# Block 3 of a three-block kernel: the cache of split weight tiles goes, and five multiplications of each recurrence element move from VectorE to GpSimd

## The reference, cut to what matters

```
h = x @ w_in + b_in                       # 1024 -> 4608 columns: 4 x 512 attention, 5 x 512 recurrence
q_a, k_a, v_a, g_a, q_h, z_fwd, z_bwd, i_h, g_h = split(h)
o_a = neighbourhood_attention(q_a, k_a, v_a, rpb) * silu(g_a)     # 8 heads, windows on a grid of 64 columns
for z in (z_fwd, z_bwd):                                          # 4 heads, forwards and backwards
    f = lb + (1 - lb) * sigmoid(z);  k = 1 - f;  b = cumsum(log f)
    o += hgrn2_chunk_scan(q_h, k, i_h, log f)
    # S_t = diag(f_t) S_(t-1) + k_t outer v_t;  o_t = S_t^T q_t, done in chunks:
    # a[t, s] = sum_d q[t, d] * exp(b[t, d] - b[s, d]) * k[s, d]  for s <= t
y = concat(o_a, rms(o) * gain * silu(g_h)) @ w_out + b_out
out = layer_norm(x * alpha + y)
```

## Time and profile before

| | us |
|---|---|
| median of 3 runs (lowest, highest) | 4557.69 (4555.84, 4560.75) |
| the profiled execution: its time, its span | 4560.75, 4558.9 |
| busy over the span: PE, DVE, ACT, POOL | 4255.9, 2695.0, 1808.8, 654.2 |
| mean granted clock of PE | 0.969 |

### The profile page before, as it was taken

One profiled execution on the slowest core, in us unless ns is written; L12 is line 12 of the kernel. 1 busy time (PEld: TensorE's weight loads), 2 busy tenths in 40 slices (PEclk: granted clock), 3 DMA queues, 4 the chain that ended last, 5 costly groups with the idle time before them and its releaser, 6 DMA issues.

```text
span 4558.9 us, 62157 instructions
## 1 busy us (share of the span) xinstructions
PE 4255.9 (93%) x24340; PEld 3457.5 (76%) x24372; DVE 2695.0 (59%) x4207; ACT 1808.8 (40%) x3435; POOL 654.2 (14%) x305
## 2 busy tenths in 40 slices
PE   7999999999899989999899979888999999899689
PEld 4888888889788877788677758767887777777467
DVE  5688888871566533044467667466354564376665
ACT  5111111111566631122466547455353453266453
POOL 2111111110333311111022112322000000000111
PEclk9999999999999999999999989999999999999789
DMA  4111111122544421111589862577664655654653
GB/s 170 51 51 51 51 51 51 51 72 91 188 131 128 129 92 49 65 59 63 188 259 290 272 255 93 177 226 257 221 206 166 198 185 169 205 188 150 207 188 129
DMA packets 515372, 663.95 MB, mean 146 GB/s; under 512 B 60348, under 2 KB 407296, under 8 KB 491658
## 3 DMA queue, kind: packets, MB, share of 16 engines
q1 hardware_dynamic: 466046, 576.89, 38.8%
q10 hardware_dynamic: 49036, 83.09, 4.9%
HBM read 442.24 MB, written 217.65 MB: 145 GB/s over the span
## 4 chain that ended last, share of the span: by engine, by line
PE 81%; DMA 6%; DVE 5%; SPq 3%; ACT 3%; issue 2%; POOL 1%; ACTq 0%; DVEq 0%; POOLq 0%
PE ps L226 10%; PE ps L227 10%; PE ps L228 10%; PE ps L3624 3%; PE ps L3625 3%; PE ps L3626 3%; PE ps L251 3%; PE ps L252 3%; PE ps L253 3%; PE ps L3744 2%; DMA w_split_tiles<-w 1%; PE ps L3713 1%; PE ps L239 1%; PE ps L240 1%; PE ps L241 1%
## 5 line engine op out<-in xcount | busy, mean ns | idle before, releaser
L226 PE MATMUL ps<-hh,wsplit 128*128 128x512 f32 x2048 | 821.7, 401 | 8.2 <-DVE hl L1376 4.2
L227 PE MATMUL ps<-hl,wsplit 128*128 128x512 f32 x2048 | 809.7, 395 | 0.0
L228 PE MATMUL ps<-hh,wsplit 128*128 128x512 f32 x2048 | 808.6, 395 | 0.0
L952 DVE SCALAR_TENSOR_TENSOR conv_acc<-conv_in,pcol,conv_acc 128x1024 f32<-128x1024 f32 x480 | 687.4, 1432 | 14.8
L226 PEld LDWEIGHTS ps<-hh,wsplit 128*128 128x128 f32 x2048 | 387.1, 189 | 102.3 <-issue 7.4
L227 PEld LDWEIGHTS ps<-hl,wsplit 128*128 128x128 f32 x2048 | 390.8, 191 | 91.7 <-issue 4.3
L228 PEld LDWEIGHTS ps<-hh,wsplit 128*128 128x128 f32 x2048 | 389.3, 190 | 89.3
L218 POOL TENSOR_TENSOR wsplit<-wraw,wsplit 128x1024 fp32r<-128x1024 f32 x72 | 204.9, 2856 | 1341.1 <-ACT wsplit L213 1341.1
L3624 PE MATMUL ps<-h_hi,w 128*128 128x512 f32 x896 | 374.9, 418 | 4.4 <-DVE h_lo L3422 4.4
L3625 PE MATMUL ps<-h_lo,w 128*128 128x512 f32 x896 | 357.7, 399 | 0.0
L3626 PE MATMUL ps<-h_hi,w 128*128 128x512 f32 x896 | 356.3, 398 | 0.0
(11 more groups left out here) (389 smaller groups left out, 8871.4 us busy)
## 6 DMA issues: line engine op xcount, KB each, us to landing
w<-w_split_tiles SPq DMA_DIRECT2D x108, 1024.0 KB, 5.4
wraw<-in_w_in SPq DMA_DIRECT2D x72, 512.0 KB, 3.8
w_split_tiles<-w SPq DMA_DIRECT2D x36, 1024.0 KB, 6.5
sh<-hy_ak ACTq DMA_DIRECT2D x48, 512.0 KB, 3.9
g_tiles<-b_ost SPq DMA_DIRECT2D x80, 256.0 KB, 5.5
w_raw<-in_w_in SPq DMA_DIRECT2D x36, 512.0 KB, 4.3
wo_raw<-in_w_out SPq DMA_DIRECT2D x32, 512.0 KB, 5.5
sh<-hy_ad ACTq DMA_DIRECT2D x32, 512.0 KB, 9.5
```

The lines of the kernel that those rows point to most:

```text
L226: e.matmul(p[:, :], wh, c.HH[tb][:, k, :], start=k == 0, stop=False)
L227: e.matmul(p[:, :], wh, c.HL[tb][:, k, :], start=False, stop=False)
L228: t = e.matmul(p[:, :], wl, c.HH[tb][:, k, :], start=False, stop=k == 7)
L952: e.scalar_tensor_tensor(v, a[:, h * 1024 + j:(h + 1) * 1024 + j], c.convw(j, ch), v, ALU.mult, ALU.add) \
```

## The change

The DRAM tensor of split tiles, its stores and its semaphores go. All 144 tiles are loaded raw and split by ScalarE and GpSimd, where it was 36. The five multiplications by k of each element go from VectorE to GpSimd, with a semaphore of their own (`rec_pool`) for which TensorE's products, and VectorE's next write of k, wait. The diff, without hunks that only delete declarations:

```diff
--- before.py
+++ after.py
...
@@ -2672,13 +2670,9 @@
         L.last_unit[n] = u
         if n >= 4:
             after(last[n - 4], "ld", n)
-            if n < 36:
-                before(last[n - 4] + 2, "split", n)
+            before(last[n - 4] + 2, "split", n)
 
     L.begin = [36 * tb for tb in range(4)]
-    L.first_with = {L.tiles[n][2]: n for n in range(36)}
-    for n in range(36):
-        after(max(last[n] - 1, 0), "w_st", n)
 
     L.units = [(tb, hd, d, h) for tb in range(4) for hd in range(4) for d in range(2) for h in range(2)]
     for n, (tb, hd, d, h) in enumerate(L.units):
@@ -2779,7 +2773,7 @@
     end = max(max(pre), max(post)) + 1
     L.order = []
     rank = {"split": 0, "log": 1, "div": 2, "el": 3, "sg": 4, "att_o": 1.5,
     for s in range(end):
-            "ld": 0, "w_st": 0.2, "val": 1, ...
+            "ld": 0, "val": 1, ...
         L.order += sorted(pre.get(s, []), key=lambda x: rank.get(x[0], 20))
         if s in L.begin:
@@ -2808,29 +2802,12 @@
 
 
 def w3_load(e, c, n):
-    L, s = c.b3, w3_slot(n)
+    L = c.b3
     if n >= 4:
         e.wait_ge(*L.done[L.last_unit[n - 4]])
-    if 4 <= n < 40:
-        e.wait_ge(*L.w_st[n % 4][n - 4])
-    if n < 36:
-        col = tile_col(L, n)
-        e.dma_start(L.Wraw[:, s, 1024:2048].rearrange("p (k n) -> p k n", k=8),
-                    c.A["w_in_3"][0][:, col:col + 128].rearrange("(k p) n -> p k n", p=128)).then_inc(*L.w_ld[n % 4].up(n))
-    else:
-        at = L.first_with[L.tiles[n][2]]
-        e.wait_ge(*L.w_st[at % 4][at])
-        e.dma_start(L.W[:, s, :].bitcast(F32), L.WD[at]).then_inc(*L.w_ld[n % 4].up(n))
-
-
-def w3_store(e, c, n):
-    L = c.b3
-    e.wait_ge(*L.lo[n])
-    e.dma_start(L.WD[n], L.W[:, w3_slot(n), :].bitcast(F32)).then_inc(*L.w_st[n % 4].up(n))
-
-
-def w3_ready(L, n):
-    return L.lo[n] if n < 36 else L.w_ld[n % 4][n]
+    col = tile_col(L, n)
+    e.dma_start(L.Wraw[:, w3_slot(n), 1024:2048].rearrange("p (k n) -> p k n", k=8),
+                c.A["w_in_3"][0][:, col:col + 128].rearrange("(k p) n -> p k n", p=128)).then_inc(*L.w_ld[n % 4].up(n))
 
 
 def w3_high(e, c, n):
@@ -2999,8 +2976,6 @@
         k = s[0]
         if k == "ld":
             w3_load(e, c, s[1])
-        elif k == "w_st":
-            w3_store(e, c, s[1])
         elif k == "row_ld" and s[1] >= 2:
             row_ld(s[1])
         elif k == "turn_x" and s[1] >= 4 and s[1] % 4 < 2:
@@ -3309,7 +3284,7 @@
             e.wait_ge(*c.by_act[u])
             e.tensor_scalar(f, f, L.lbv[:, a + 16 + hd:a + 17 + hd], L.lbv[:, a + 12 + hd:a + 13 + hd], ALU.mult, ALU.add).then_inc(*L.f_d.up(((tb, hd), "f", d)))
             if tb or hd:
-                e.wait_ge(*L.r_dve[first_of(tb, hd) - 4 + 2 * d + 1, "ke"])
+                e.wait_ge(*L.r_pool[first_of(tb, hd) - 4 + 2 * d + 1, "ke"])
             e.wait_ge(*L.f_d[(tb, hd), "f", d])
             e.tensor_scalar(L.KK[:, d, :], f, -1.0, 1.0, ALU.mult, ALU.add).then_inc(*L.f_d.up(((tb, hd), "k", d)))
         elif kind == "rq":
@@ -3371,15 +3346,10 @@
         to = L.QE[:, qs, :] if d else L.KE[:, s, :]
         e.tensor_tensor(v3(to, 128), v3(w, 128), end, op).then_inc(*L.r_dve.up((n, "dif", "l")))
         for lv, (B, x, kd, qsl, ksl) in enumerate(lvs):
-            e.wait_ge(*L.r_act[n, "k", lv])
-            e.tensor_tensor(kd[:, :, ksl], kd[:, :, ksl], v3(k, B)[:, :, ksl], ALU.mult).then_inc(*L.r_dve.up((n, "k", lv)))
             e.wait_ge(*L.r_act[n, "q", lv])
             e.tensor_tensor(x[:, :, qsl], x[:, :, qsl], v3(q, B)[:, :, qsl], ALU.mult).then_inc(*L.r_dve.up((n, "q", lv)))
         e.wait_ge(*L.r_act[n, "qd"])
-        e.tensor_tensor(L.KD[:, s, :], L.KD[:, s, :], k, ALU.mult).then_inc(*L.r_dve.up((n, "kd")))
         e.tensor_tensor(L.QD[:, s, :], L.QD[:, s, :], q, ALU.mult).then_inc(*L.r_dve.up((n, "qd")))
-        e.wait_ge(*L.r_act[n, "ke"])
-        e.tensor_tensor(L.KE[:, s, :], L.KE[:, s, :], k, ALU.mult).then_inc(*L.r_dve.up((n, "ke")))
         e.wait_ge(*L.r_act[n, "qe"])
         e.tensor_tensor(L.QE[:, qs, :], L.QE[:, qs, :], q, ALU.mult).then_inc(*L.r_dve.up((n, "qe")))
 
@@ -3587,6 +3557,16 @@
         k = s[0]
         if k == "split":
             w3_low(e, c, s[1])
+        elif k == "el":
+            n = s[1]
+            k = inputs_of(L, n)[1]
+            for lv, (B, x, kd, qs, ks) in enumerate(levels(L, n)):
+                e.wait_ge(*L.r_act[n, "k", lv])
+                e.tensor_tensor(kd[:, :, ks], kd[:, :, ks], v3(k, B)[:, :, ks], ALU.mult).then_inc(*L.r_pool.up((n, lv)))
+            for name, t in (("kd", L.KD), ("ke", L.KE)):
+                v = t[:, n % 2, :]
+                e.wait_ge(*L.r_act[n, "qd" if name == "kd" else "ke"])
+                e.tensor_tensor(v, v, k, ALU.mult).then_inc(*L.r_pool.up((n, name)))
         elif k == "wo_split":
             for q in range(s[1], s[1] + 4):
                 e.wait_ge(*L.wo_hi[q])
@@ -3618,15 +3598,14 @@
         e.wait_ge(*c.by_dve["x", 4 * tb + 3, 1])
         s = w3_slot(n)
         if u[0] == "col":
-            e.wait_ge(*w3_ready(L, n))
+            e.wait_ge(*L.lo[n])
             for k in range(8):
                 wh, wl = L.W[:, s, k * 128:(k + 1) * 128], L.W[:, s, 1024 + k * 128:1024 + (k + 1) * 128]
                 e.matmul(p[:, :], wh, L.HH[:, k, :], start=k == 0, stop=False)
                 e.matmul(p[:, :], wh, L.HL[:, k, :], start=False, stop=False)
                 t = e.matmul(p[:, :], wl, L.HH[:, k, :], start=False, stop=k == 7)
         else:
-            e.wait_ge(*w3_ready(L, n))
-            e.wait_ge(*w3_ready(L, n + 1))
+            e.wait_ge(*L.lo[n + 1])
             for i in range(2):
                 ts, out = slice(128 * (u[5] + i), 128 * (u[5] + i) + 128), p[:, 256 * i:256 * i + 256]
                 for k in range(8):
@@ -3644,6 +3623,7 @@
         for lv, (B, x, kd, qs, ks) in enumerate(levels(L, n)):
             h = B // 2
             e.wait_ge(*L.r_dve[n, "q", lv])
+            e.wait_ge(*L.r_pool[n, lv])
             for bl in range(256 // B):
                 i = bl * B % 128
                 k0 = i + ks.start if B > 32 else i
@@ -3654,12 +3634,13 @@
         e.matmul(p, c.zb[:, 0:128], c.zb[:, 0:256], start=False, stop=True)
         p = both[:, 256:512]
         e.wait_ge(*L.r_dve[n, "qd"])
+        e.wait_ge(*L.r_pool[n, "kd"])
         for j in range(2):
             ps = slice(j * 128, (j + 1) * 128)
             t = e.matmul(p[:, ps], L.KD[:, s, ps], L.QD[:, s, ps], start=True, stop=True)
         t.then_inc(*L.r_pe.up((n, "diag")))
         p = take_bank(e, c, ("kv", n), L.rb)
-        e.wait_ge(*L.r_dve[n, "ke"])
+        e.wait_ge(*L.r_pool[n, "ke"])
         for j in range(2):
             ps = slice(j * 128, (j + 1) * 128)
             t = e.transpose(p[:, ps], L.KE[:, s, ps], c.ident)
```

More of the change, by code:

```diff
@@ L2560, in b3_layout @@
     L.QED, L.KVD, L.OD = dram("chain_q_rows", 4, 128, S_LEN), dram("chain_kv_rows", 4, 128, S_LEN), dram("rec_o_rows", 4, 128, S_LEN)
-    L.WD = c.nc.dram_tensor("w3_split_tiles", (36, 128, 2048), F32, kind="Internal").ap()
     L.RD, L.BD = dram("rpb_rows", 120, 128), dram("bias_rows", 2, 4, 128, 1152)
@@ L2572, in b3_layout @@
     L.hi, L.lo, L.done = sig("w3_hi"), sig("w3_lo"), sig("b3_projected")
-    L.w_st = [dsig(f"w3_split_st{i}") for i in range(4)]
     L.tr, L.h_hi = sig("x2_turned"), sig("h3_hi")
@@ L2580, in b3_layout @@
     L.f_a, L.f_d = sig("forget_by_act"), sig("forget_by_dve")
-    L.r_pe, L.r_act, L.r_dve = sig("rec_pe"), sig("rec_act"), sig("rec_dve")
+    L.r_pe, L.r_act, L.r_dve, L.r_pool = sig("rec_pe"), sig("rec_act"), sig("rec_dve"), sig("rec_pool")
     L.qe_st, L.kv_st, L.o_st = [dsig(f"chain_q_st{i}") for i in range(4)], [dsig(f"chain_kv_st{i}") for i in range(2)], [dsig(f"rec_o_st{i}") for i in range(2)]
@@ L2781, in b3_order @@
     rank = {"split": 0, "log": 1, "div": 2, "el": 3, "sg": 4, "att_o": 1.5,
-            "ld": 0, "w_st": 0.2, "val": 1, "turn": 2, "qk": 3, "bias": 4, "out": 0.3, "state": 0.4, "prod": 3.5, "y_ld": 7, "ch_o": 8, "sq": 8.2, "o_root": 8.4, "chain": 9, "o_sum": 9.5, "o": 10, "o_end": 11, "y_split": 12, "o_norm": 13, "fin": 19, "o_st": 24, "x_ld": 25, "ch_ld": 26, "values": 27}
+            "ld": 0, "val": 1, "turn": 2, "qk": 3, "bias": 4, "out": 0.3, "state": 0.4, "prod": 3.5, "y_ld": 7, "ch_o": 8, "sq": 8.2, "o_root": 8.4, "chain": 9, "o_sum": 9.5, "o": 10, "o_end": 11, "y_split": 12, "o_norm": 13, "fin": 19, "o_st": 24, "x_ld": 25, "ch_ld": 26, "values": 27}
     for s in range(end):
```

## The result

| | before | changed |
|---|---|---|
| median of 4 runs, us | 4558.28 | 4593.75 (4592.61 to 4598.52) |
| the profiled execution, its span | 4560.75, 4558.9 | 4597.2, 4595.4 |
| time block 0 | 312.4 | 289.8 |
| time block 1 | 289.1 | 297.5 |
| time block 2 | 334.2 | 343.8 |

The ratio is 1.0078, 95% interval 1.0065 to 1.0090: slower by 35 us, as forecast (4599, +41). The block times are read from the trace, from the first matmul of the in-projection in one time block to the first of the next (the last: to the end of slot 143). By this measure the blocks of the kernel before begin at 2915.4, 3227.8, 3516.9 and 3851.1 us, and its 144 slots take 1302 us, 9.0 each. Before time block 0 the changed kernel has 0.9 us more.

The account below looks back on a forecast made before the run. TensorE sets the pace, with SyncE's queue, held by stores, pacing block 0. Terms −20 + 21 + 39 − 3 + 4 = +41 us gave 4602 against 4560.75, or 4599 against the median; range 4534 to 4650.

Parts of the forecast that it names:

- A, stores: Block 0: the 36 stores go, raw loads no longer wait for them; −20 us, bounds −34 and −5.
- R4: Rival, block 0: stores were no limit, bursts keep tiles late, gain only −5 us; 4614, chance 0.08.
- Price on GpSimd: Small multiplications on GpSimd: 0.43 us for 128 columns, 0.71 for 256, 2.7 us an element.
- The element: Element on VectorE beside GpSimd's multiplications: +1.1 us each, bounds −1.7 and +2.4.
- The subtract: GpSimd's 1024-column subtract holds VectorE up to 2.4 us; in block 3, twelve of 16 element slots have a split.
- R2: Rival: only the small multiplications collide, the subtract lands after the scaling; −2 us, 4556, chance 0.15.
- B: Blocks 1 and 2, 32 elements: delays expose the softmax scaling to TensorE; +21 us, bounds 0 and +50.
- C: Block 3, closed loop of 16 element slots: longer element and subtract delay the scaling; +39 us, bounds +8 and +60.
- D: Traffic: loads of 0.5 MB in place of 1 MB; −3 us, bounds 0 and −15.
- E: Block 3: ScalarE's 1.06 us copy behind the last exponential, exposed in four slots; +4 us, bounds 0 and +17.
- R1: Rival: GpSimd's work fits in beside VectorE, which loses 114 us of its own work; −32 us, 4526, chance 0.18.
- R3: Rival: a backlog, GpSimd and VectorE wait for each other and gaps lower TensorE's clock; +105 us, 4663, chance 0.11.

Follow-up runs that it names:

- the better order: Changed kernel with the weight split ahead of the softmax exponential, in its old slot: 4557.45 us, ratio 0.9986 to the kernel before.
- two edits in the order: Changed kernel with multiplications by k after those by q, and the split ahead of the softmax exponential in its old slot: 4533.42 us, again 4531.00.

## Why the prediction was right, point by point

The time came out by the forecast's mechanism: GpSimd's work beside VectorE makes VectorE late, and TensorE waits for the softmax scaling. The sizes inside the sum were less well met than the sum.

*A, stores.* −20 expected, −22.6 measured. 12 of it is the waiting queue, by the run with the earlier store. The rest is open between less traffic, which I had put at −3 and elsewhere, and what the stores still hold up. Not as forecast is the picture of the loads: they didn't come closer together, but one to a slot, and it is only behind a burst that they now catch up at once. R4 (the stores are no limit) is out.

*Price on GpSimd.* 0.43 and 0.71 us from a line through 512 and 1024 columns; measured 0.61 and 0.79 beside VectorE, 0.49 and 0.76 out of its way. That is 3.4 us an element where 2.7 was forecast.

*The element.* +1.1 us was taken between −1.7 and +2.4; with only the multiplications moved it is +0.7. The rule that each small operation blocks too is right for the durations: 282 becomes 703. The cost of +2.4 is wrong, and so is the upper bound with it: where VectorE waits for each of them in turn it has still lost five operations of its own, so the bound is 2.7 − 1.7 = +1.0, or +1.7 with the measured 3.4. The +1.1 itself was borrowed from collisions of another kind, those with the subtract in block 0, so its nearness to 0.7 is partly luck. The Trainium skill, "SBUF — State Buffer", section "Who interferes with whom", adds that an instruction of VectorE with at most one SBUF input, outside the two-port modes, doesn't contend; the trace agrees (555 ns at most in the 74 reductions and 559 in the 31 additions beside a subtract), and on this the better order rests.

*The subtract.* 2.4 us on twelve of sixteen elements of block 3: the count is exact, and the place wasn't: in all twelve it fell on the element's last multiplication, not on the scaling. That is because the small collisions delayed VectorE; where they are absent, in the kernel that has no cache and k on VectorE, it falls on the scaling. R2, the subtract behind the scaling, is out.

*B.* +21 expected, +18.0 measured; 12.8 us of it stand in the trace as TensorE's waits for the scaling (none before). The 9.6 us of a slot took in what follows the last slot; it is 9.0, which changes nothing in the sum.

*C.* With D and E +39 + 4 − 3 = +40 expected, +37.9 measured, and here the nearness is partly luck. The sum spoke of waits alone, about 40 us more of them for the scaling. They grew by 16.5 (1.9 to 18.4), the idle time as a whole by 24.5, and the other 13.4 are the same matmuls at a clock of 0.95 in place of 0.97, for which C had no term; only R3 had one. Of the eight logarithm scalings put at 6 us one was long (2023 ns), 1.5 us. That half of the loss comes only when both parts of the change are there wasn't forecast either.

*R1* is out for this kernel, but two edits in the order bring it about, as its sum had it: almost all of the gain in block 0 and nearly none in blocks 1 to 3, 4533 where it had 4526. *R3*: no backlog, GpSimd works 1126.8 − 654.2 = 473 us more in the whole (518 − 36 x 2.4 = 432 forecast).
